# Half a unit of the next stage's projection ahead of the meeting at four seams of a two-layer encoder

## The chip, the cores and the metric

The kernel runs on one core of one Trainium2 chip. It is written by hand, one program for each engine, with semaphores between them. The metric is the device time of one launch in microseconds (us); the smaller, the better. Several runs are taken and their median counts.

## The reference

Two layers of an encoder over 1024 tokens of 1024 channels. Each layer projects the normalized input with one wide matrix `w_in` (1024 x 8464) and feeds three branches from it: windowed attention (a), differential attention over the full sequence (b), and a gated delta rule in both directions behind a short convolution (c). The three outputs are gated and merged.

```python
for l in range(DEPTH):                       # 2
    h = rmsnorm(x, norm_g[l])
    proj = einsum('bsd,de->bse', h, w_in[l])
    (a_q, a_k, a_v, a_z, b_q, b_k, b_v, b_z,
     c_qkv, c_z, c_b, c_a, gate_logits) = split(proj, offsets)
    o_a = windowed_gqa(a_q, a_k, a_v, a_sink[l], cos, sin)     # 8 heads, window 128
    y_a = (o_a * silu(a_z)) @ w_bo_a[l]
    o_b = diff_attention(b_q, b_k, b_v, lam, b_subln_g[l], lam_init, cos, sin)
    y_b = (o_b * silu(b_z)) @ w_bo_b[l]
    c_q, c_k, c_v = split(silu(centred_short_conv(c_qkv, c_conv_w[l])), 3)
    # beta and g from c_b, c_a; unit length for q and k
    o_c = rmsnorm(gated_delta_chunked(forward) + flip(gated_delta_chunked(backward)))
    y_c = (o_c * silu(c_z)) @ w_bo_c[l]
    gates = sigmoid(gate_logits)             # three of 1024 channels
    merged = gates[0] * y_a + gates[1] * y_b + gates[2] * y_c
    x = x + merged @ w_out[l]
return rmsnorm(x, final_g)
```

## The kernel before, in words

**Stages.** A layer is a chain of six blocks of code, one function each: `project(l)`, `attend_window(l)` (names with `win`), `attend_full(l)` (`diff`), `prepare(l)` (`prep`), `delta_rule(l)` (`delta`) and `merge_output(l)`. A small stage that loads x stands ahead of layer one, and one for the last norm behind layer two. Inside a block every engine has a program of its own (sync for DMA queues, gpsimd, tensor, scalar, vector). All engines meet at a block's end, and no engine starts on the next block before; in the profile TensorE's sequencer shows this at line 203. The four seams that the change touches are those from `project` to `attend_window`, from there to `attend_full`, on to `prepare`, and on to `delta_rule`.

**Units and halves.** Only the first columns of `proj` are made by `project`. The rest is cut in units of 128 columns (`U_BQ + k`, `diff_unit`, the gates' units), and TensorE makes them in the stages between, among each stage's own work ("side" work, class `Side`, lines 221 to 294). A unit for all 1024 tokens is two halves of 512 tokens. A half is 8 slices of the contraction, with three matmuls each, since float32 is computed as a sum of products of a high and a low part: 24 matmuls of 128x512 (`part`, line 266). The steps of a unit:
- `load`: SyncE loads the 1024 x 128 weights into `w_stage[k % 2]`.
- `split`: GpSimd makes `w_hi[k % 2]` (line 246) and `w_lo[k % 2]` (line 251), in four pieces each. In `prepare`, ScalarE makes the high part (`high`, line 1805) and GpSimd the low part (`low`, line 1691).
- `half`, or `part` slice by slice: TensorE accumulates a half in a bank of PSUM. It waits for `side_lo` (the unit is split) and for `side_out`: the half before it in the same bank has been read.
- `out`: ScalarE copies the bank into `ev[k % 2]` (line 281), and after a unit's second half issues its store to `proj` (line 285).

The last two units that a stage splits (`ahead=True`, or the numbers UNITS and above) belong to the next stage, which finds their semaphores set ahead by the numbers in `AHEAD`; with `SIDE_AHEAD_IN`, only one counts as split. `project` works on pairs of units of its own kind; its last loads and splits are those of the two units that `attend_window` begins with, and that stage's `split(1)` makes the second of them once more. The halves of `attend_window` and `attend_full` all go through bank 7 (`banks=(7, 7)`); in `prepare` and `delta_rule` the first half of a unit goes through bank 6 and the second through bank 7.

**TensorE's order in each stage.** The order is written out by hand; nothing is planned at run time.
- `attend_window`: halves 0 and 1, `turn_values` (transposes of the values, line 917), halves 2 and 3, then the steps: `scores(n)` (line 934), side parts, `turn`, `sum_values`, ... and `LAST` = 3 halves behind the last steps. GpSimd's order is split(1), three sines (`sine(r)`, line 883), split(2), and so on. `FIRST` = 4 counts the halves ahead of the steps.
- `attend_full`: `FIRST` = 3 halves, then steps of `scores(n)` (line 1317), side parts, `turn`, `sum_values` (line 1357); `LAST` = 5 halves at the end, between which `sum_squares` stands. The keys' parts that the scores read are made by ScalarE (`high`, line 1396) and VectorE (`low`, line 1505).
- `prepare`, for each of four heads: halves, `total` (sums of squares, line 1728), a half, `total`, halves, `products`, `turn` of k, a half, `turn` of v (line 1743), halves. ScalarE begins with high(1) and with a `tanh` (line 1774) among its evictions; GpSimd begins with low(1).
- `delta_rule`: `EARLY` = 10 halves, then four stages of `blocks` (line 2082) that solve the triangular systems from `delta_u` and its like, which are loaded back from memory (line 1962).

## Time and profile before

| | us |
|---|---|
| median of 3 runs | 2816.32 (2814.8 to 2816.42) |
| the profiled execution, its own time | 2818.19 |
| its span in the profile | 2816.4 |
| TensorE busy | 2684.4 (95%) |
| VectorE / GpSimd / ScalarE busy | 1473.7 / 1199.6 / 1153.8 |
| mean granted TensorE clock | 0.982 of full speed |

How to read it: times are microseconds from the span's start. PE is TensorE's matmuls, PEld its weight loads (which overlap them), PEq its sequencer; DVE is VectorE, ACT ScalarE, POOL GpSimd, and SPq or ACTq the DMA issues of SyncE or ScalarE. L266 is line 266 of the kernel. An operation is written out<-in, with the names of the program's buffers.

### The profile page before, as it was taken

How to read it: one execution, taken by the hardware profiler on the slowest of the kernel's cores; microseconds unless marked ns; L12 is line 12 of the kernel's file. 1: busy time of each engine (PE TensorE's matmuls, PEld its weight loads, DVE VectorE, ACT ScalarE, POOL GpSimd, SP SyncE). 2: the span in 40 equal slices, each digit the busy share in tenths (PEclk: the TensorE clock that was granted, in tenths of full speed). 3: DMA queues.
4: the chain of work that ended last, by engine and by line, in shares of the span. 5: the costliest groups of instructions: out<-in, count | busy, mean ns of one | idle time of the engine just before them, and what ended most of it. 6: DMA issues, size and time to landing. Idle time of an engine off the chain costs nothing. (4 is left out here: it accounts for less than half of the span.)

```text
span 2816.4 us, 39100 instructions
## 1 busy us (share of the span) xinstructions
PE 2684.4 (95%) x15158; PEld 2143.7 (76%) x15158; DVE 1473.7 (52%) x1835; ACT 1153.8 (41%) x1914; POOL 1199.6 (43%) x1108
## 2 busy tenths in 40 slices
PE   8989999999999999999999999899999999999998
PEld 4867767777778789878767777677777887897786
DVE  5136527777467343476240555277764764335752
ACT  3124424666365414342121344266663653244311
POOL 2464335443365450253434653444433654303633
PEclk9999999999999999999999999999999999999999
DMA  6253224231355555754243532433224564567532
GB/s 210 92 150 98 90 80 125 90 98 68 120 184 185 187 156 155 233 187 129 83 153 105 143 104 69 123 97 98 83 68 135 191 197 160 164 161 257 158 120 105
DMA packets 394072, 380.89 MB, mean 135 GB/s; under 512 B 90144, under 2 KB 332448, under 8 KB 393888
## 3 DMA queue, kind: packets, MB, share of 16 engines
q1 hardware_dynamic: 354912, 296.39, 34.8%
q10 hardware_dynamic: 38976, 82.00, 7.9%
q8 instruction: 121, 1.98, 0.3%
q14 instruction: 63, 0.52, 0.1%
HBM read 248.22 MB, written 130.09 MB: 134 GB/s over the span
## 5 line engine op out<-in xcount | busy, mean ns | idle before, releaser
L266 PE MATMUL pair<-h_hi,w_hi 128*128 128x512 f32 x1792 | 740.2, 413 | 75.0 <-PEq L203 39.9
L266 PE MATMUL pair<-h_lo,w_hi 128*128 128x512 f32 x1792 | 708.5, 395 | 0.0
L266 PE MATMUL pair<-h_hi,w_lo 128*128 128x512 f32 x1792 | 708.3, 395 | 0.0
L246 POOL TENSOR_TENSOR w_hi<-w_stage,masks 128x256 fp32r<-128x256 f32 x312 | 257.5, 855 | 642.7 <-PE pair L266 604.7
L266 PEld LDWEIGHTS pair<-h_hi,w_hi 128*128 128x128 f32 x1792 | 342.4, 191 | 197.0 <-issue 83.3
L266 PEld LDWEIGHTS pair<-h_hi,w_lo 128*128 128x128 f32 x1792 | 342.4, 191 | 75.6
L266 PEld LDWEIGHTS pair<-h_lo,w_hi 128*128 128x128 f32 x1792 | 343.3, 192 | 70.2 <-issue 5.3
L281 ACT ACTIVATE ev<-pair 128x512 f32<-128x512 f32 x224 | 132.8, 593 | 456.7 <-PE pair L266 455.7
L251 POOL TENSOR_TENSOR w_lo<-w_stage,w_hi 128x256 fp32r<-128x256 f32 x312 | 247.3, 823 | 6.1
L1691 POOL TENSOR_TENSOR w_lo<-w_stage,w_hi 128x256 fp32r<-128x256 f32 x128 | 149.5, 1197 | 170.5 <-ACT w_hi L1805 170.5
L1446 ACT ACTIVATE diff_p<-pair,diff_stat 128x1024 f32<-128x1024 f32 x128 | 142.9, 1117 | 126.4 <-DVE diff_stat L1549 122.4
L217 PE MATMUL pair<-h_hi,w_hi 128*128 128x512 f32 x512 | 158.5, 391 | 0.0
L217 PE MATMUL pair<-h_lo,w_hi 128*128 128x512 f32 x512 | 157.8, 389 | 0.0
L217 PE MATMUL pair<-h_hi,w_lo 128*128 128x512 f32 x512 | 157.6, 389 | 0.0
L1549 DVE TENSOR_REDUCE diff_stat<-pair 128x1 f32<-128x1024 f32 x128 | 150.1, 1214 | 1.3 <-PE pair L1317 1.0
L2401 POOL TENSOR_TENSOR w_lo<-w_stage,w_hi 128x512 fp32r<-128x512 f32 (+1 forms) x60 | 125.9, 2098 | 57.7 <-ACT w_hi L2458 54.2
L2399 POOL TENSOR_TENSOR w_hi<-w_stage,masks 128x512 fp32r<-128x512 f32 (+1 forms) x44 | 77.4, 1758 | 168.3 <-PE pair L217 147.7
L1032 ACT ACTIVATE win_s<-win_s,small 128x385 f32<-128x385 f32 (+1 forms) x128 | 74.7, 585 | 103.4 <-DVE small L1112 103.4
L1511 DVE TENSOR_TENSOR diff_a_lo<-pair,diff_a_hi 128x1024 fp32r<-128x1024 f32 x64 | 78.2, 1222 | 73.3 <-ACT diff_a_hi L1468 63.1
L535 POOL TENSOR_TENSOR w_hi<-w_stage,masks 128x1024 fp32r<-128x1024 f32 x20 | 47.6, 2381 | 157.0 <-PE pair L217 145.8
L1575 DVE SCALAR_TENSOR_TENSOR diff_p<-diff_p,diff_stat,diff_p 128x1024 f32<-128x1024 f32 x64 | 89.0, 1390 | 45.9 <-ACT diff_p L1455 45.7
L217 PEld LDWEIGHTS pair<-h_hi,w_hi 128*128 128x128 f32 x512 | 95.5, 188 | 21.3 <-issue 1.7
(288 smaller groups left out, 4894.7 us busy)
## 6 DMA issues: line engine op xcount, KB each, us to landing
w_stage<-in_w_in SPq DMA_DIRECT2D x132, 512.0 KB, 4.2
proj<-ev ACTq DMA_DIRECT2D x132, 512.0 KB, 2.7
gate<-proj SPq DMA_DIRECT2D x48, 512.0 KB, 3.7
prep_x<-proj SPq DMA_DIRECT2D x24, 512.0 KB, 4.1
resid<-xT SPq DMA_DIRECT2D x16, 512.0 KB, 6.2
diff_vx<-proj SPq DMA_DIRECT2D x16, 512.0 KB, 3.2
prep_g<-gc_rows SPq DMA_DIRECT2D x16, 512.0 KB, 5.0
qd_t<-prep_eg SPq DMA_DIRECT2D x16, 512.0 KB, 2.6
```

What stands on the lines that cost most here:

```text
L217: last = nc.tensor.matmul(pair[0:m, half, :], lhs[:, k, 0:m], rhs[:, k, half * HALF:(half + 1) * HALF], start=(k == 0 and n == 0), stop=(k ...
L246: last = nc.gpsimd.tensor_tensor(w_hi[s][:, part], w_stage[s][:, part], bcast(ones, PIECE), ALU.mult)
L251: last = nc.gpsimd.tensor_tensor(w_lo[s][:, part], w_stage[s][:, part], w_hi[s][:, part].bitcast(F32), ALU.subtract)
L266: last = nc.tensor.matmul(bank(self.banks[half]), a[s][:, c, :], b[:, c, w], start=(c == 0 and n == 0), stop=(c == KC - 1 and n == 2))
L281: nc.scalar.activation(ev[s][:, half * HALF:(half + 1) * HALF], bank(self.banks[half]), ACT.Tanh if gate else ACT.Copy, scale=0.5 if gate ...
L1446: nc.scalar.activation(p[c][:], flat(pairs[c]), ACT.Exp, bias=st[:, 0, c:c + 1], accum_out=st[:, 2, c:c + 1]).then_inc(q["exped"], 1)
L1511: nc.vector.tensor_tensor(a_lo[:, :, w], by_tile(pairs[2]), a_hi[:, :, w].bitcast(F32), ALU.subtract)\
L1549: nc.vector.tensor_reduce(st[:, 0, c:c + 1], flat(pairs[c]), AX_X, ALU.max, negate=True)\
L1575: nc.vector.scalar_tensor_tensor(out=p[0][:], in0=p[1][:], scalar=st[:, 4, 0:1], in1=p[0][:], op0=ALU.mult, op1=ALU.add).then_inc(q["mixed ...
L1691: last = nc.gpsimd.tensor_tensor(w_lo[s][:, part], w_stage[s][:, part], w_hi[s][:, part].bitcast(F32), ALU.subtract)
L2399: nc.gpsimd.tensor_tensor(hi, stage, bcast(ones, kc), ALU.mult).then_inc(q[f"w_hi{s}"], 1)
L2401: nc.gpsimd.tensor_tensor(lo, stage, hi.bitcast(F32), ALU.subtract).then_inc(q[f"w_lo{s}"], 1)
```

## The change

TensorE makes half 0 of the next stage's first unit at the end of the stage before, ahead of the meeting: a new function `lead`. The next stage's ScalarE evicts it first. The bank that holds it is given to `Side` as the first of `early`, and the first few halves of `attend_window` and `attend_full` go round three banks. `AHEAD` is changed so that each of the four stages finds both of its first two units split and one half summed. Where the stage before split one unit for the next (`attend_full`, `prepare`) it now splits two; the next stage's own split of unit 1 goes, and `FIRST` and `LAST` move by one.

```diff
+SIDE_AHEAD = {"side_in0": 16, "side_in1": 16, "side_hi": 2, "side_lo": 2, "side_sum": 1}
-AHEAD["win"] = SIDE_AHEAD_IN          (likewise "prep" and "delta"; "diff" had SIDE_AHEAD)
+AHEAD["win"] = dict(SIDE_AHEAD)
...
 class Side:
-    def __init__(self, l, q, per, banks=(7, 7)):
+    def __init__(self, l, q, per, banks=(7, 7), early=()):
+        self.bank_of = lambda n: early[n] if n < len(early) else banks[n % 2]
...
     part: (matmul and eviction use bank(self.bank_of(2 * k + half)))
+        n = 2 * k + half
+        late = 0 if self.bank_of(n) == self.bank_of(n - 1) else 1
+        pe.wait_ge(q["side_out"], START + turn * (2 * self.per) + max(n - late, 0))
...
+def lead(pe, into):
+    for c in range(KC):
+        for n, (a, b) in enumerate(((w_hi, h_hi), (w_hi, h_lo), (w_lo, h_hi))):
+            nc.tensor.matmul(bank(into), a[0][:, c, :], b[:, c, 0:HALF], start=(c == 0 and n == 0),
+                             stop=(c == KC - 1 and n == 2))
+LEAD_WINDOW, LEAD_FULL, LEAD_GATES = 6, 0, 6
 # project, TensorE, at the end
+    pe.wait_ge(q["w_lo0"], START + pairs_of_units + 1)
+    lead(pe, LEAD_WINDOW)
 # attend_window
-side = Side(l, q, UNITS)
+side = Side(l, q, UNITS, early=(LEAD_WINDOW, 7, 5, 7, 5))
-FIRST, LAST = 4, 3
+FIRST, LAST = 5, 2
-    split(1)                                   (GpSimd, ahead of the sines)
-    side_half(0)
     side_half(1); turn_values(); side_half(2); side_half(3)
+    side_half(4)
...
-    side_half(tail_half(2))
+    pe.wait_ge(q["side_lo"], START + UNITS + 1)
+    lead(pe, LEAD_FULL)
 # attend_full
+side = Side(l, q, UNITS, early=(LEAD_FULL, 7, 5, 7))
-FIRST, LAST = 3, 5
+FIRST, LAST = 4, 4
+    split(17)                                  (GpSimd, at the end)
-    for n in range(FIRST): side_half(n)
+    for n in range(1, FIRST): side_half(n)
...
-    side_half(tail_half(4))
+    pe.wait_ge(q["side_lo"], START + UNITS + 1)
+    lead(pe, LEAD_GATES)
     (ScalarE)
-    for n in range(2): side_out(n); high(0, n)
-    side_out(2)
+    side_out(0)
+    for n in range(2): side_out(n + 1); high(0, n)
+    side_out(3)
 # prepare: GpSimd low(1) and ScalarE high(1) go from the start, low(17) and high(17) stand at the end
-    half(0); half(1); h == 0: half(2), half(3)
+    h > 0: half(0), half(1); h == 0: halves 1 to 4
     total(h, 1)
-    half(2 if h else 4)
+    half(2 if h else 5)
     total(h, 0)
-    half(3 if h else 5); half(4 if h else 6)
+    half(3 if h else 6); h > 0: half(4)
     products(h); turn of k
-    h > 0: half(5)
+    half(5 if h else 7)
     turn of v
-    h > 0: half(6); half(7)
+    h > 0: half(6), half(7)
+pe.wait_ge(q["side_lo"], START + PREPARED + 1)
+pe.wait_ge(q["side_out"], START + 2 * PREPARED - 1)
+lead(pe, LEAD_GATES)
 # prepare, ScalarE, head 0: the halves' evictions follow the new order
-    out_half(0, 0); ...; tanh; ...; out_half(0, 3); ...; out_half(h, 4); out_half(h, 5)
+    out_half(0, 0); ...; tanh; ...; out_half(0, 3); ...; out_half(0, 4); ...; out_half(0, 5)
 # delta_rule
-    for k in range(1, N_GATE - PREPARED): split   (GpSimd)
+    for k in range(2, N_GATE - PREPARED): split
-    for n in range(EARLY): side_half(n)
+    for n in range(1, EARLY): side_half(n)
+    side_out(0)                                (ScalarE, first of all)
```

## Rows read from the trace of the kernel before

**Rows 1.** The page, part 1: busy time of each engine, share, instructions.

```profile
PE 2684.4 (95%) x15158; PEld 2143.7 (76%) x15158; DVE 1473.7 (52%) x1835; ACT 1153.8 (41%) x1914; POOL 1199.6 (43%) x1108
```

**Rows 2.** Waits of TensorE: waiting line <- releaser: total, times, longest.

```profile
PE pair L266 <- PEq L203: 39.9, 8, 6.2
PE pair L266 <- ACT ev L281: 29.2, 34, 3.9
...
PE pair L1743 <- ACT k_tok L1800: 2.4, 2, 1.2
```

**Rows 3.** Three windows: length, busy by engine, granted clock, DMA share, GB/s.

```profile
151.77:157.83 6.06, 6.06 (x14) 4.78 (x15) 0.00 (x0) 0.00 (x0) 2.07 (x3) 0.50 0.89 205
185.10:188.55 3.45, 3.45 (x8) 2.80 (x9) 0.83 (x2) 1.56 (x2) 3.37 (x5) 0.51 0.54 152
1540.07:1543.64 3.57, 3.57 (x9) 2.80 (x10) 0.00 (x0) 0.00 (x0) 0.00 (x0) 0.50 0.81 186
```

**Rows 4.** Time line of TensorE, seam one: start, duration, line, operation, [idle before].

```profile
151.77 0.77 PE L266 MATMUL pair<-h_hi,w_hi 128*128 128x512 f32 x1 [5.44 <-PEq L203]
...
166.62 1.03 PE L917 MATMUL pair<-masks,win_vx 128*128 128x128 f32 x8
...
180.84 0.38 PE L934 MATMUL pair<-win_hi,win_hi 64*128 64x256 f32 x2
...
185.10 0.80 PE L266 MATMUL pair<-h_hi,w_hi 128*128 128x512 f32 x1 [3.65 <-POOL w_lo L251]
```

**Rows 5.** Time line of GpSimd, seam one.

```profile
148.90 2.34 POOL L538 TENSOR_TENSOR w_lo<-w_stage,w_hi 128x1024 fp32r<-128x1024 f32 x1
...
161.53 3.87 POOL L883 TENSOR_TENSOR win_xr<-win_xr,sin 128x256 f32<-128x256 f32 x4
...
176.43 5.77 POOL L246 TENSOR_TENSOR w_hi<-w_stage,masks 128x256 fp32r<-128x256 f32 x4
```

**Rows 6.** The tile win_vx, its instructions and DMA to landing.

```profile
L1012 ACTq DMA_DIRECT2D win_vx<-proj x1: 445/445/445, 153.5 to 153.5; - x1
...
DMA to landing us min/median/max: 11.3/11.3/11.3
```

**Rows 7.** Time line of all engines, seam two.

```profile
412.94 2.76 POOL L246 TENSOR_TENSOR w_hi<-w_stage,masks 128x256 fp32r<-128x256 f32 x4 [7.47 <-PE pair L266]
...
419.04 0.76 PE L266 MATMUL pair<-h_hi,w_hi 128*128 128x512 f32 x1 [6.18 <-PEq L203]
...
437.12 1.25 DVE L1505 TENSOR_TENSOR diff_k_lo<-diff_xk,diff_k_hi 128x1024 fp32r<-128x1024 f32 x1 [1.13 <-ACT diff_k_hi L1396]
...
439.05 2.81 POOL L251 TENSOR_TENSOR w_lo<-w_stage,w_hi 128x256 fp32r<-128x256 f32 x4
...
440.02 0.73 PE L1317 MATMUL pair<-diff_k_hi,diff_q_hi 64*128 64x512 f32 x4
...
441.61 0.50 PE L266 MATMUL pair<-h_hi,w_hi 128*128 128x512 f32 x1
```

**Rows 8.** Time line of all engines, seam three.

```profile
755.55 0.60 ACT L281 ACTIVATE ev<-pair 128x512 f32<-128x512 f32 x1 [5.82 <-PE pair L266]
...
759.48 0.76 PE L266 MATMUL pair<-h_hi,w_hi 128*128 128x512 f32 x1 [3.97 <-PEq L203]
...
770.46 1.06 ACT L1774 ACTIVATE prep_t<-k_all 128x1024 f32<-128x1024 f32 x1 [0.54 <-DVE k_all L1888]
...
775.63 5.86 POOL L1691 TENSOR_TENSOR w_lo<-w_stage,w_hi 128x256 fp32r<-128x256 f32 x4 [12.35 <-ACT w_hi L1805]
...
784.11 1.88 PE L1728 MATMUL pair<-prep_t,masks 128*128 128x512 f32 x4
```

**Rows 9.** Time line of all engines, seam four.

```profile
977.92 0.77 PE L266 MATMUL pair<-h_hi,w_hi 128*128 128x512 f32 x1 [3.96 <-PEq L203]
...
1030.99 1.91 ACTq L1962 DMA_DIRECT2D delta_u<-solved  x4
...
1035.32 0.60 PE L2082 MATMUL pair<-delta_t,delta_qm 64*32 64x32 f32 x32
```

More of the change, by code:

```diff
@@ L152, in build_program @@
             "qd_put1"] + SIDE)
-        AHEAD["delta"] = SIDE_AHEAD_IN
+        AHEAD["delta"] = dict(SIDE_AHEAD)
         SIGNALS["delta"] = (["w_raw_in", "w_in", "zeroed", "w_set", "w_copied", "w_scaled", "w_solved", "kept",
@@ L222, in build_program @@
         class Side:
-            def __init__(self, l, q, per, banks=(7, 7)):
-                self.q, self.per, self.banks = q, per, banks
+            def __init__(self, l, q, per, banks=(7, 7), early=()):
+                self.q, self.per = q, per
+                self.bank_of = lambda n: early[n] if n < len(early) else banks[n % 2]
                 self.in_slot = [(per + 1 - s) // 2 for s in range(2)]
@@ L260, in part @@
                 if c == 0:
-                    late = 0 if self.banks[0] == self.banks[1] else 1
-                    pe.wait_ge(q["side_out"], START + turn * (2 * self.per) + max(2 * k + half - late, 0))
+                    n = 2 * k + half
+                    late = 0 if self.bank_of(n) == self.bank_of(n - 1) else 1
+                    pe.wait_ge(q["side_out"], START + turn * (2 * self.per) + max(n - late, 0))
                 w = slice(half * HALF, (half + 1) * HALF)
                 for n, (a, b) in enumerate(((w_hi, h_hi), (w_hi, h_lo), (w_lo, h_hi))):
-                    last = nc.tensor.matmul(bank(self.banks[half]), a[s][:, c, :], b[:, c, w], start=(c == 0 and n == 0),
+                    last = nc.tensor.matmul(bank(self.bank_of(2 * k + half)), a[s][:, c, :], b[:, c, w], start=(c == 0 and n == 0),
                                             stop=(c == KC - 1 and n == 2))
@@ L280, in out @@
                 act.wait_ge(q["side_sum"], START + turn * (2 * self.per) + (2 * k + half + 1))
-                nc.scalar.activation(ev[s][:, half * HALF:(half + 1) * HALF], bank(self.banks[half]), ACT.Tanh if gate else ACT.Copy,
+                nc.scalar.activation(ev[s][:, half * HALF:(half + 1) * HALF], bank(self.bank_of(2 * k + half)), ACT.Tanh if gate else ACT.Copy,
                                      scale=0.5 if gate else scale).then_inc(q["side_out"], 1)
@@ L890, in split @@
                             side.split(pool, 1, k - UNITS, ahead=True)
-                    split(1)
                     for r in range(3):
@@ L1154, in attend_full @@
                 UNITS = 4 * HEADS
-                side = Side(l, q, UNITS)
+                side = Side(l, q, UNITS, early=(LEAD_FULL, 7, 5, 7))
                 side_unit = lambda k: diff_unit(k // 4, k % 4)
@@ L1295, in _ @@
                     split(16)
+                    split(17)
                 @block.tensor
@@ L1359, in sum_squares @@
                         last.then_inc(q["total"], 1)
-                    for n in range(FIRST):
+                    for n in range(1, FIRST):
                         side_half(n)
@@ L1697, in mask @@
                         nc.gpsimd.tensor_tensor(G[d][:], G[d][:], bcast(beyond(d), NT), ALU.add).then_inc(q["masked"], 1)
-                    low(1)
                     for h in range(4):
@@ L1717, in _ @@
                         low(4 * h + 4)
+                    low(17)
                 @block.tensor
@@ L1747, in _ @@
                         half = lambda n: side.half(pe, 0, 4 * h + n // 2, n % 2)
-                        half(0)
-                        half(1)
-                        if h == 0:
-                            half(2)
-                            half(3)
+                        if h:
+                            half(0)
+                            half(1)
+                        else:
+                            for n in range(1, 5):
+                                half(n)
                         total(h, 1)
-                        half(2 if h else 4)
+                        half(2 if h else 5)
                         total(h, 0)
-                        half(3 if h else 5)
-                        half(4 if h else 6)
+                        half(3 if h else 6)
+                        if h:
+                            half(4)
                         products(h)
@@ L1809, in out_half @@
                         side_out(act, m)
-                        if m % 2 and (m + 3) // 2 <= PREPARED:
+                        if m % 2:
                             high((m + 3) // 2)
-                    high(1)
                     for h in range(4):
@@ L1831, in _ @@
                         to_exp(1, h)
-                        out_half(h, 2 if h else 4)
+                        if h:
+                            out_half(h, 2)
                         out_half(h, 3 if h else 5)
@@ L2050, in _ @@
                     last.then_inc(q["zeroed"], 1)
-                    for k in range(1, N_GATE - PREPARED):
+                    for k in range(2, N_GATE - PREPARED):
                         side.split(pool, 0, k)
@@ L2105, in blocks @@
                         last.then_inc(q["levels"], 1)
-                    for n in range(EARLY):
+                    for n in range(1, EARLY):
                         side_half(n)
@@ L2196, in _ @@
                     nc.scalar.activation(W[:, 1], RAW1, ACT.Copy).then_inc(q["w_copied"], 1)
-                    for n in range(EARLY):
+                    for n in range(1, EARLY):
                         if n == EARLY - 1:
```

24 lines of the change are left out of this document (9 added, 15 removed).

## The prediction

> **What bounds the kernel now.** I read the page first: TensorE is busy for 2684.4 of 2816.4 us, no other engine for more than 1474 [rows 1]. So TensorE's order of work is the path, and a change pays only by its pauses (132 us in all) or its clock. The view of waits then says where the pauses are [rows 2]: 39.9 us in 8 pauses behind the meetings of the engines (the sequencer's line 203), up to 6.2 each; 29.2 in 34 for a ScalarE eviction; and small ones, such as 2.4 for k_tok. Third, the windows behind those pauses: TensorE's granted clock is 0.50 of full speed, that is 1.2 instead of 2.4 GHz, for 6.06 us after the 5.44 us meeting pause, for 3.57 us after its twin in layer two, and for 3.45 us after a 3.65 us pause [rows 3]. Half of such a stretch is lost: 3.0, 1.8, 1.7 us. Last, the time lines of all engines around the four seams of layer one, to see which engine ended the stage and what TensorE waits for behind the meeting. The second layer repeats them.
>
> **What every seam gains and what it costs.** The change moves one half (24 matmuls) ahead of each of the four meetings of a layer. Such a half takes 5.45 us at full clock: ten of them between 977.92 and 1035.32 are 57.4 us, less 3.0 for the half clock, by ten [rows 9]. The number of matmuls in the program stays the same; what changes is pauses. Behind a meeting that TensorE ends itself, it should pause about 0.5 us: at the first seam GpSimd's split ended at 151.24 (148.90 + 2.34) and TensorE resumed at 151.77 [rows 4, 5]. But the half that is moved was also the filler under which the next stage's loads and splits ran. So each seam has to be followed until the next stage's own data stand in the way. I call the moment at which TensorE resumes r.
>
> **Seam one, projection to window attention.** Before, TensorE ends at 146.33 (151.77 - 5.44). The lead half runs until 151.8, next to the split which ends at 151.24, so r moves by +0.5 to 152.3. Behind r TensorE has halves 1, the turn of the values, 2, 3, 4 and then the scores. The values' load is issued at 153.5 and lands 11.3 us later, at 164.8 [rows 6], 165.3 after; TensorE is there at 157.8 and pauses 7.5 us, where before half 0 and half 1 covered it (turn at 166.62). It does the turn and two halves until about 180 and then wants unit 2, which GpSimd splits behind its three sines, from 176.43 on, and TensorE waited for it before too, until 185.10 [rows 4, 5]. Taking split(1) out of GpSimd's queue doesn't bring this forward. It ended just ahead of the first sine, at 161.53, whose input had landed just then (VectorE's cosine on the same input starts with it), and the later sines wait for their loads as well; I take 0, and the bound below is a split 5.7 us earlier (its cost), which no load supports. So half 4 starts at 185.6 against 185.1, and the scores of step 0 (0.6 us), done before in the cover of that pause, now stand behind it: 0.5 + 0.6 lost. The pause ahead of it grows from 3.65 to some 5.8 us; behind it I take 2.2 us lost to the half clock (between the rows' 1.8 and 3.0) against 1.7. Sum -1.6 us per layer, ends 0 and -3. The 5.44 us pause and its 3.0 us of half clock are gone, but come back as the pauses for values and unit 2.
>
> **Seam two, window to full attention.** Before: TensorE ends at 412.86 (419.04 - 6.18) and GpSimd's split of unit 17 only starts there (412.94), 5.6 us. After: that split starts at half 31's end and runs beside the values' sum (1.1 us) and the lead (5.45), 6.5 in all; the pause falls from 6.18 to 0.5, +5.7. Behind r before: three halves (one at half clock, two evictions waited for), scores at 440.02 = r + 21.0 [rows 7]. After: three halves on three banks take 16.4 us; but the low part of k comes from loads, sine, rotation and split: 437.12 + 1.25 = 438.4, r + 19.3. So a new pause of 2.9 us, then 1.6 us of scores (440.02 to 441.61), then half 4, whose unit GpSimd ends at 439.05 + 2.81 = 441.86 = r + 22.8 (it waited 0.4 for TensorE's half; 22.4 after). Before, half 3 started at 441.61 = r + 22.6. So +0.2 there, less 0.4 for what the clock may take: +5.5 per layer, ends +3.5 and +6.5.
>
> **Seam three, full attention to preparation.** Before, TensorE ends at 755.51 and ScalarE's eviction (755.55 + 0.60) and its store make the meeting wait: pause 3.97 [rows 8]. After, the store runs under the lead, and GpSimd's added split(17) starts with it: twice 2.8 us, the price of a split in rows 7, or 5.7 against 5.45; the pause is 0.8, +3.2. Halves 30 and 31 have the sum of squares between them, which hides an eviction wait of 0.75: it is among the 34 [rows 2]. Behind r before: four halves, total at 784.11 = r + 24.6. After: half 1 and 2 until r + 10.9; half 3 wants bank 7, which ScalarE empties only behind the tanh that starts at 770.46, r + 12.7: pause 1.8. Half 4 is of unit 2: its high part follows at r + 14.2, the low part takes GpSimd 5.86 beside VectorE's taps, r + 20.1: pause 2.0. Total at r + 25.5, 0.9 later. One half then stands between the turns of k and v, and the k_tok wait (2.4 in 2) goes: +1.2. Sum +4.2, ends +2 and +5.5.
>
> **Seam four, preparation to delta rule.** Pause 3.96 to 0.5: +3.4, and the 3.0 of half clock go. But this stage begins with halves 0 to 9 and then needs the solved blocks: VectorE's chain, a round trip through memory, and ScalarE's loads 1030.99 + 1.91 = 1032.90, landing some 1.5 us later, about r + 56.5 [rows 9]. TensorE came at r + 57.4, just behind. With nine halves it comes at r + 49.1. ScalarE, no longer held by half 8, can issue up to 1.6 us earlier: inputs at r + 55, pause 5.9 us, and 2.2 of half clock behind. Before: 3.96 + 3.0 = 7.0 of pause and clock; after: 0.5 + 5.9 + 2.2 = 8.6. So -1.7 per layer, ends 0 and -3.
>
> One rule bears on this. The rows show half clock behind the pauses of 3.65 and 5.44 us and full clock through the busy stretches [rows 3, 4]. The Trainium skill ("TensorE: Matmul & The Clock Gate", "HAM oscillation — how this bites in real kernels") has it that loads waited for between groups of matmuls make each group start slow, and its advice is to order the work so that the engine stays busy. By that the lead is right where it closes the pause and worth nothing where the pause only moves; the first of these, at every seam, is the first rival below.
>
> **Other edits at nothing.** Three early banks instead of one: the gain stands in seams two and three; the early evictions cost ScalarE the same 0.6 us each. Taking out high(1) and low(1) in the preparation and split(1) in the delta rule frees engines that nobody waits for there; what went in ahead of the meeting was counted at seam three, and at seam four high(17), low(17) is 0.6 + 0.5 + 1.06 + 2.8 = 5.0 us under a lead of 5.45 (if weights 17 came late it would cost their delay). The side work in the steps runs one half ahead and with the other parity; TensorE's waits there are evictions of 1.2 us and less, so I take 0, ends -2 and +2.
>
> **Sum.** Per layer -1.6 + 5.5 + 4.2 - 1.7 = 6.4; two layers 12.8, say 13. The profiled execution took 2818.19 us (span 2816.4 and 1.8 around it), so 2805.2; it stands 1.9 above the median of 2816.32, hence 2803.3 for the median.
>
> **Rivals.** (a) Full price: all eight pauses close to 0.5 (36 us), the half clock behind them is gone (about 2.7 each, 21), evictions too (5): 62 us, 2754. For it: rows 2. Against it: the loads and splits of seams one and four are just in time already. 4%. (b) Chain: slower. In window attention the first scores come 13 us later (194 against 181). If the chain scores, exp, turn, sum bounded this stage, its end would move by that, -26 in two layers, against the +16 that seams two to four bring: 2826. It decides from the point where that chain takes longer than a step of TensorE; against it, no wait for exp or turn stands among TensorE's large ones. 7%. (c) The new pauses of seams two and three each put TensorE at half clock (1.7 us, three times per layer) or the ends of seams one and four hold: gain about 3, 2813. 20%. (d) The pauses of seams one and four are milder, nothing lost there: gain 19, 2797. 15%. (e) The lead isn't done in the meeting's shadow, since something else holds TensorE (a split that its wait names comes late): the pause moves ahead of the lead, 0 to -5: 2818. 2%. My forecast, 2798 to 2809: 52%.
>
> Faster by over 0.2% (2810.7 and below; less than that can't be told from no change): 0.52 + 0.15 + 0.04 and a fifth of (c): 0.76. Same: the rest of (c) and half of (e), 0.16. Slower: 0.08. The range leaves out (a), (b) and the outer ends of (c) and (d): 2793 to 2815; the forecast's own is 2798 to 2809.
>
> **What would show it.** Line 266's waits for the meetings fall from 39.9 us to under 8. New in the waits: line 917 for the load of win_vx, 7 us in each layer; line 266 for w_lo by line 251, 6 us in each; line 2082 for the delta inputs, 5 to 6 in each; line 1317 for the low part of k, 3 in each; line 266 for w_lo by line 1691, 2 in each. Half clock behind the meetings is gone but stands behind the first three of these. The forecast is wrong if seam two's meeting doesn't come 5 us earlier, or if split(2) in window attention ends well ahead of TensorE.

## The result, and the profile after

The changed kernel takes 2832.33 us (median of 5 runs, 2828.0 to 2840.16) against 2816.32 (2814.8 to 2819.97, 5 runs): ratio 1.0061, 95% interval 1.0044 to 1.0078. It is slower by some 17 us where 13 us faster was forecast, and outside the range. Its profiled execution took 2837.72 us (span 2835.9), 5.4 above its median.

Line numbers below are mostly of the changed kernel: its lines 268, 252, 283, 1705, 1742 and 2098 are 266, 251, 281, 1691, 1728 and 2082 of the kernel before. First the page, part 1, of the changed kernel, for [rows 1]:

```profile
PE 2683.5 (95%) x15158; PEld 2143.0 (76%) x15158; DVE 1478.3 (52%) x1835; ACT 1153.4 (41%) x1914; POOL 1169.8 (41%) x1092
```

TensorE's busy time is the same (2684.4 before) with as many matmuls; the pauses are 152 us where they were 132. The waits of TensorE after, for [rows 2]:

```profile
PE pair L268 <- ACT ev L283: 24.1, 22, 1.7
PE pair L268 <- POOL w_lo L252: 22.1, 7, 6.2
PE pair L928 <- DMA win_vx<-proj: 13.8, 2, 6.9
PE pair L1742 <- ACT prep_t L1796: 9.8, 2, 4.9
PE pair L2098 <- DMA delta_u<-solved: 9.5, 2, 5.9
...
PE pair L1330 <- DVE diff_k_lo L1519: 6.2, 2, 3.1
PE pair L268 <- POOL w_lo L1705: 5.9, 4, 1.6
...
PE pair L268 <- PEq L203: 3.5, 8, 1.0
```

The meetings' 39.9 us are 3.5, as meant. In their place stand five waits that were forecast (win_vx, w_lo of unit 2, diff_k_lo, w_lo by line 1705, delta_u) and one that was not: 4.9 us in each layer for prep_t. Of the 22.1 us for w_lo by line 252, 4.7 (unit 7 of the window stage, in both layers) and 2.0 (a unit of the gates in layer two's delta rule) weren't forecast either, and of the 5.9 by line 1705, 1.36 in each layer (the second head's first half). Where they fall shows in the windows of the four stages, from one meeting to the next (columns as in [rows 3]); first the kernel before, then the changed one, layer one:

```profile
151.77:419.04 267.27, 253.30 (x1321) 191.25 (x1321) 129.01 (x198) 100.99 (x236) 127.35 (x160) 0.98 0.35 105
419.04:759.48 340.44, 323.37 (x1840) 258.66 (x1841) 224.50 (x273) 199.75 (x277) 145.93 (x155) 0.99 0.29 94
759.48:977.92 218.44, 213.26 (x992) 172.98 (x993) 133.44 (x101) 118.53 (x173) 114.12 (x80) 0.98 0.59 188
977.92:1174.00 196.08, 188.39 (x1873) 165.29 (x1873) 84.10 (x190) 68.17 (x166) 50.52 (x72) 0.98 0.57 165
```

```profile
153.03:424.25 271.22, 254.44 (x1321) 192.23 (x1321) 128.21 (x198) 100.76 (x236) 123.53 (x152) 0.97 0.34 103
424.25:763.14 338.89, 320.24 (x1840) 256.99 (x1841) 225.21 (x268) 199.84 (x276) 139.10 (x163) 1.00 0.30 94
763.14:985.73 222.59, 212.92 (x992) 171.40 (x993) 136.27 (x103) 118.33 (x173) 115.16 (x80) 0.99 0.58 185
985.73:1181.07 195.34, 181.51 (x1849) 159.04 (x1849) 83.39 (x190) 68.27 (x166) 44.74 (x64) 0.98 0.58 165
```

The first three stages do as many halves as before (each gives one away and takes one over) and end in a meeting that costs 3 to 6 us less, so each should be shorter. But window attention is 4.0 us longer and the preparation 4.2; only full attention is shorter, by 1.6. The delta rule, which does one half less (24 matmuls, 5.45 us), is 0.7 shorter. In layer two the four differences are +3.3, +0.2, +4.8 and +3.3. The last is not typical: of eight kernels below with the same delta rule seven took 192.7 to 195.1 us there, one 198.2, this one 199.1.

**Window attention, in the middle.** GpSimd and TensorE of the changed kernel, time line:

```profile
256.89 4.03 POOL L895 TENSOR_TENSOR win_xr<-win_xr,sin 128x256 f32<-128x256 f32 x4 [8.87 <-DMA win_xr<-proj]
260.88 2.83 POOL L247 TENSOR_TENSOR w_hi<-w_stage,masks 128x256 fp32r<-128x256 f32 x4
263.79 3.88 POOL L252 TENSOR_TENSOR w_lo<-w_stage,w_hi 128x256 fp32r<-128x256 f32 x4
...
267.72 0.50 PE L268 MATMUL pair<-h_hi,w_hi 128*128 128x512 f32 x1 [2.26 <-POOL w_lo L252]
```

And GpSimd at the same place before:

```profile
250.32 3.90 POOL L883 TENSOR_TENSOR win_xr<-win_xr,sin 128x256 f32<-128x256 f32 x4 [9.25 <-DMA win_xr<-proj]
...
258.07 2.94 POOL L251 TENSOR_TENSOR w_lo<-w_stage,w_hi 128x256 fp32r<-128x256 f32 x4
```

GpSimd's last sine waits for a load in both kernels, and the split of unit 7 is queued behind it. Before, that split ended 6 us ahead of its use (261.01 and 266.99). The sine's load goes with the stage's steps, and with 5 halves instead of 4 ahead of the steps they begin a half later: the sine starts 6.6 us later and the split ends 6.7 us later (267.67), while TensorE wants the unit 1.5 us sooner (265.46).

**Full attention, in the steps.** The other parity moves GpSimd's gating (line 1280) from behind a split (572.37 in the trace before, behind the split that starts at 564.81) to beside VectorE's mixing (line 1589):

```profile
564.99 2.40 POOL L1280 TENSOR_TENSOR diff_o<-diff_o,diff_zt 128x1024 f32<-128x1024 f32 x1 [2.42 <-DVE diff_o L1536]
565.27 3.20 DVE L1589 SCALAR_TENSOR_TENSOR diff_p<-diff_p,diff_stat,diff_p 128x1024 f32<-128x1024 f32 x1
...
572.52 0.50 PE L268 MATMUL pair<-h_hi,w_hi 128*128 128x512 f32 x1 [1.02 <-ACT ev L283]
```

VectorE's operation has a median of 1.28 us over its 64 places and takes 3.20 here: it ends 1.08 us behind GpSimd's (568.47 and 567.39), as if it had hardly begun before. The maximum, the exp and the eviction behind it are late, and TensorE pauses 1.02 us where it paused 0.16. This happens twice per layer.

**Preparation, second head.** ScalarE, SyncE and TensorE of the changed kernel, three stretches of the time line (the first row of the first and of the last is of the first head):

```profile
782.52 1.06 ACT L1796 ACTIVATE prep_t<-k_all 128x1024 f32<-128x1024 f32 x1
...
827.61 1.06 ACT L1823 ACTIVATE w_hi<-w_stage 128x1024 fp32r<-128x1024 f32 x1 [9.59 <-DMA w_stage<-in_w_in]
829.47 1.05 ACT L1792 ACTIVATE prep_t<-prep_yq 128x1024 f32<-128x1024 f32 x1
830.42 1.05 ACT L1796 ACTIVATE prep_t<-k_all 128x1024 f32<-128x1024 f32 x1
```

```profile
822.77 0.43 SPq L237 DMA_DIRECT2D w_stage<-in_w_in  x1
```

```profile
788.70 1.88 PE L1742 MATMUL pair<-prep_t,masks 128*128 128x512 f32 x4
...
831.52 1.14 PE L1742 MATMUL pair<-prep_t,masks 128*128 128x512 f32 x1 [4.93 <-ACT prep_t L1796]
```

And ScalarE and TensorE in the kernel before, at the same place:

```profile
825.41 1.05 ACT L1778 ACTIVATE prep_t<-k_all 128x1024 f32<-128x1024 f32 x1
...
827.05 1.45 PE L1728 MATMUL pair<-prep_t,masks 128*128 128x512 f32 x3
```

Before, the square was ready at 826.46 and TensorE came at 827.05: no pause, but a margin of 0.6 us, and no view of waits shows a margin. From the meeting on, TensorE did ten halves ahead of this total. Now one of them is done ahead of the meeting and nine are left, while the square comes at r + 68.3 instead of r + 67.0 (r is TensorE's start in the stage, 763.14 and 759.48). TensorE itself is there at 826.59, r + 63.4 instead of r + 67.6. So of the pause 4.1 us are the missing half and 1.3 the later square, less the margin of 0.6.

**The clock.** Five windows right behind pauses of the changed kernel (values, unit 2, unit 7, prep_t, delta_u):

```profile
165.59:167.60 2.01, 2.01 (x9) 2.01 (x10) 1.23 (x1) 0.39 (x1) 1.60 (x2) 0.50 1.08 277
185.17:190.10 4.93, 4.93 (x12) 3.91 (x13) 0.00 (x0) 0.00 (x0) 4.85 (x8) 0.52 0.38 106
267.72:271.50 3.78, 3.78 (x10) 2.99 (x11) 3.12 (x5) 2.46 (x6) 3.78 (x4) 0.59 0.68 171
831.52:835.20 3.68, 3.68 (x5) 1.60 (x6) 3.61 (x4) 2.98 (x4) 1.67 (x2) 0.54 1.14 350
1041.13:1046.00 4.87, 4.87 (x42) 3.94 (x43) 0.00 (x0) 1.07 (x4) 0.00 (x0) 0.50 0.79 205
```

The first stretch goes on at 0.50 to 169.48, 3.89 us in all. So each of these pauses brings its own stretch at or near 1.2 GHz: 1.5 to 2.4 us lost (the length times one less the granted clock). The one of only 2.26 us, ahead of unit 7, costs 1.5 of that. The Trainium skill ("TensorE: Matmul & The Clock Gate", "HAM oscillation — how this bites in real kernels") has waits for loads between groups of matmuls make the next group start at the low clock, and the trace agrees.

### The profile page after: what moved, and what is told of

Same layout as the page of the kernel before. It is cut to its first block and busy times, and to the rows that moved or that the text cites. A ratio compares the mean times of both kernels' runs of the same rounds, so it can differ in the third digit from the quotient of the medians.

```text
span 2835.9 us, 39076 instructions
## 1 busy us (share of the span) xinstructions
PE 2683.5 (95%) x15158; PEld 2143.0 (76%) x15158; DVE 1478.3 (52%) x1835; ACT 1153.4 (41%) x1914; POOL 1169.8 (41%) x1092
## 5 line engine op out<-in xcount | busy, mean ns | idle before, releaser
L268 PE MATMUL pair<-h_hi,w_hi 128*128 128x512 f32 x1728 | 712.9, 413 | 56.7 <-ACT ev L283 24.1
L268 PE MATMUL pair<-h_lo,w_hi 128*128 128x512 f32 x1728 | 680.5, 394 | 0.0
L268 PE MATMUL pair<-h_hi,w_lo 128*128 128x512 f32 x1728 | 680.4, 394 | 0.0
L247 POOL TENSOR_TENSOR w_hi<-w_stage,masks 128x256 fp32r<-128x256 f32 x304 | 245.3, 837 | 586.5 <-PE pair L268 536.5
L268 PEld LDWEIGHTS pair<-h_hi,w_hi 128*128 128x128 f32 x1728 | 328.5, 190 | 173.5 <-issue 63.4
L268 PEld LDWEIGHTS pair<-h_hi,w_lo 128*128 128x128 f32 x1728 | 328.6, 190 | 72.7
L268 PEld LDWEIGHTS pair<-h_lo,w_hi 128*128 128x128 f32 x1728 | 329.2, 191 | 68.4 <-issue 6.3
L252 POOL TENSOR_TENSOR w_lo<-w_stage,w_hi 128x256 fp32r<-128x256 f32 x304 | 222.1, 762 | 6.0
L1705 POOL TENSOR_TENSOR w_lo<-w_stage,w_hi 128x256 fp32r<-128x256 f32 x128 | 150.1, 1202 | 165.0 <-ACT w_hi L1823 165.0
L217 PE MATMUL pair<-h_hi,w_hi 128*128 128x512 f32 x512 | 158.4, 391 | 0.0
L217 PE MATMUL pair<-h_lo,w_hi 128*128 128x512 f32 x512 | 157.7, 389 | 0.0
L217 PE MATMUL pair<-h_hi,w_lo 128*128 128x512 f32 x512 | 157.7, 389 | 0.0
L1589 DVE SCALAR_TENSOR_TENSOR diff_p<-diff_p,diff_stat,diff_p 128x1024 f32<-128x1024 f32 x64 | 97.1, 1517 | 46.1 <-ACT diff_p L1470 46.0
L1119 DVE SCALAR_TENSOR_TENSOR win_s<-pair,band 128x768 f32<-128x768 f32 (+1 forms) x64 | 56.9, 890 | 109.3 <-PE pair L945 109.2
```

The lines of the kernel that those rows point to most:

```text
L217: last = nc.tensor.matmul(pair[0:m, half, :], lhs[:, k, 0:m], rhs[:, k, half * HALF:(half + 1) * HALF], start=(k == 0 and n == 0), stop=(k ...
L247: last = nc.gpsimd.tensor_tensor(w_hi[s][:, part], w_stage[s][:, part], bcast(ones, PIECE), ALU.mult)
L252: last = nc.gpsimd.tensor_tensor(w_lo[s][:, part], w_stage[s][:, part], w_hi[s][:, part].bitcast(F32), ALU.subtract)
L268: last = nc.tensor.matmul(bank(self.bank_of(2 * k + half)), a[s][:, c, :], b[:, c, w], start=(c == 0 and n == 0), stop=(c == KC - 1 and n ...
L1589: nc.vector.scalar_tensor_tensor(out=p[0][:], in0=p[1][:], scalar=st[:, 4, 0:1], in1=p[0][:], op0=ALU.mult, op1=ALU.add).then_inc(q["mixed ...
L1705: last = nc.gpsimd.tensor_tensor(w_lo[s][:, part], w_stage[s][:, part], w_hi[s][:, part].bitcast(F32), ALU.subtract)
```

## The experiments

All ratios are to the kernel before, run beside each kernel on the same chip; its medians there were 2813.6 to 2816.6 us. Every kernel does the whole computation.

**One seam at a time.** Each has the lead at one seam, with what the change did in the stages on its two sides; the rest is as before.

> The lead half at seam one alone (projection to window attention), with the window stage's own order of halves as before (4 halves ahead of the steps, 3 behind). Theory A (what seam one gives is what the forecast said, and the loss in the middle of the window stage comes from the half that the steps run ahead, which this kernel does not do): the pauses for the values (7 us) and for unit 2 (about 6 us) stand in place of 5.44 us, 0.75 and 3.65, nothing waits in the middle: +0 to +3 us for both layers, 2816 to 2819. Theory B (the new pauses cost what they cost in the changed kernel, w_lo pause near 268 us included): +6 to +9, 2822 to 2825.

> The lead half at seam two alone (window to full attention), with the full attention stage as in the changed kernel. Theory A: the meeting's pause falls from 6.2 to 0.3 us, 0.6 us is lost ahead of the first scores, and about 2.2 us in each layer to evictions in the steps that come late in the new parity: about 3.7 us gained per layer, 2809. The forecast's own size for this seam: 5.5 per layer, 2805. Theory B (the gain shows nowhere, since a later chain takes it back): 2816.

> The lead half at seam three alone (full attention to preparation). Theory A (the preparation is bound at the second head's total by the chain of VectorE and ScalarE, which starts at the meeting: TensorE had just enough halves to cover it, and the half done ahead is one less): the pause of 4 us goes at the meeting but 4.9 us come back at the second head's total with half clock behind it, and the meeting itself is 5.45 - 3.3 later: 3 to 5 us lost per layer, 2822 to 2826. The forecast's size (+4.2 gained per layer): 2808.

> The lead half at seam four alone (preparation to delta rule). The forecast's size: 1.7 us lost per layer, 2820, with a pause of some 6 us for delta_u in each layer. Theory A: the same for the pause, and in one layer or the other 1 to 3 us more behind it (a late split of the gate units, or late step values): 2819 to 2825. Rival: nothing lost at all, since the pause replaces the meeting's one for one: 2816.

| lead at | ratio | 95% interval | us, both layers | forecast |
|---|---|---|---|---|
| seam one | 1.0003 | 0.9994 to 1.0013 | +1 | +3 |
| seam two | 0.9982 | 0.9971 to 0.9993 | -5 | -11 |
| seam three | 1.0039 | 1.0024 to 1.0055 | +11 | -8 |
| seam four | 1.0014 | 1.0005 to 1.0024 | +4 | +3 |

The us are (ratio - 1) x 2815. The sum is +11. The forecast has seams one and four right; seam two gives half of it; seam three has the wrong sign. Theory A is nearest at all four; seam two gives a little less than it says and seam three costs a little more. In the kernel with seam three alone the windows of the two stages (full attention, preparation) read

```profile
420.35:763.80 343.45, 329.53 (x1864) 263.49 (x1864) 225.02 (x268) 199.71 (x276) 151.56 (x163) 0.99 0.29 93
763.80:984.57 220.77, 207.52 (x968) 167.02 (x969) 136.13 (x103) 117.23 (x172) 112.28 (x76) 0.99 0.58 186
```

Full attention is 3.0 us longer, with a half more (5.45) and the cheaper meeting. The preparation does a half less and is still 2.3 us longer than before.

**The window stage's order.**

```diff
 # split7_first, GpSimd           # window_4_3
 split(6)                         -FIRST, LAST = 5, 2
+split(7)                         +FIRST, LAST = 4, 3
 sine(5)                          (half 4 in the steps, one more half at the end)
-split(7)
```

> The changed kernel, but GpSimd splits unit 7 of the window stage ahead of its last sine (it stood behind it). Theory A (the 2.3 us pause of TensorE in the middle of the window stage, at 267.7 and 1660.9 in the trace of the changed kernel, is this split, late behind the sine since the steps run one half ahead; half clock of 1.7 us follows): both pauses go, 8 us less than the changed kernel, ratio to the kernel before about 1.003 (the changed one had 1.0061). Rival (the unit's weights or the buffer come late, not the order): the pause stays, 1.006.

> The changed kernel, but with 4 halves ahead of the window stage's steps and 3 behind, as before, so that the steps do not run one half ahead. Theory A: the same pauses in the middle go by the other way, and the first scores fall back into the cover of the pause for unit 2 (0.6 us more): 8 to 9 us less than the changed kernel, ratio 1.003. Rival (the loss in the middle comes from the gain at the seam itself): 1.006.

Measured: 1.0040 (1.0027 to 1.0053) and 1.0035 (1.0022 to 1.0048) against the changed kernel's 1.0061. The pauses at 267.7 and 1660.9 are gone in both profiles. The intervals overlap a little with the changed kernel's (1.0044 to 1.0078), but two different edits that remove the same two pauses agree: the order in the steps cost 6 to 7 us in all. With the four seams' 11 that is the 17 us measured.

**The preparation: three trials that missed, one that hit in part.**

```diff
 # prep_shifted: every half from head 0's end on one place earlier (TensorE, ScalarE)
 # weights5_first, SyncE, head h > 0
+weights(4 * h + 1)
 put_queries(h - 1); load(h + 1, 1); put_products(h - 1, 0)
-weights(4 * h + 1)
 # squares_first, ScalarE
 square(1, 1)
+high(5)                           (stood behind half 7's eviction)
```

> The changed kernel, but in the preparation TensorE does every half from head 0's end on one place earlier (half 8 behind head 0's turns, halves 9 and 10 ahead of the second head's first total, and so on), so that as many halves lie ahead of that total as before the change. Theory A (the chain of ScalarE and VectorE sets that total, and a half fewer lay ahead of it): the pauses of 4.9 us and the half clock behind them (1.5 us) go, 13 us less than the changed kernel, ratio 1.0015. Rival (the halves, one place earlier, wait for their own splits, high parts behind ScalarE's tanh and low parts behind GpSimd's masks): the pause is split over several, 1.004 to 1.006.

> The changed kernel, but in the preparation SyncE issues the load of unit 4h+1's weights ahead of its other issues for head h (it stood behind the stores of the products of the head before). Theory C (the pause of 4.9 us at the second head's total is this load: it is issued at 822.8 behind seven stores that wait for VectorE's product, lands at 827.5, ScalarE's high part of unit 5 waits for it, and the tanh and the square that TensorE's total needs stand behind it on ScalarE): the load goes out at about 815.5, lands by 821, the square is done when VectorE's convolution and silu are (about 826.9), TensorE pauses under 0.6 us there; 12 us less than the changed kernel, ratio to the kernel before 1.002 (the changed one 1.0061). Theory A as first put (VectorE's and ScalarE's own work is the chain): the pause stays, 1.006.

> The changed kernel, but ScalarE makes the high part of unit 5 in the preparation behind the square of the second head's k instead of ahead of it; the load stays where it was. Theory C: the total's input is ready at about 827 as well, so the pause of 4.9 us goes, but unit 5 is now split later: its half (the third of the second head) may wait 1 us; 10 to 12 us less than the changed kernel, ratio 1.002 to 1.0025. Theory A: no change, 1.006.

Measured: 1.0099 (1.0084 to 1.0114), 1.0047 (1.0033 to 1.0060), 1.0073 (1.0059 to 1.0086). With one more half ahead of the total, that half waits 5.9 us for unit 5's low part and two more waits of 1.3 appear. With the square first, the pause goes to the same half:

```profile
PE pair L268 <- POOL w_lo L1705: 16.7, 6, 5.4
...
PE pair L1742 <- ACT prep_t L1796: 0.6, 2, 0.3
```

With the load first the wait for prep_t falls from 9.8 to 3.9 us, yet the kernel gains some 4 us where 12 were expected, and the intervals overlap. So the load was one link and not the whole cause: behind it ScalarE waits for VectorE's convolution.

> seams_1_2_3, but in the preparation's first head both totals stand one half earlier (behind halves 3 and 4, as many halves into the stage's own order as before the change), and ScalarE takes the first root ahead of half 4's eviction. Theory E (the square is ready at 20.4 us into the stage, the total waits until 25.5 behind half 4, which waits for its split; from there the chain of roots, decays and products is late until the second head): the chain moves forward by up to 5 us, the pauses at the second head's total (2.0 and 1.6 us and their half clock, about 5 us per layer) shrink: ratio 0.992 to 0.9935. Rival (VectorE is busy without a break from the first head's silu to the second head's, so its own work sets the second head's total): 0.995 as seams_1_2_3.

> The changed kernel with one edit: the preparation's first head does both totals one half earlier (and ScalarE its first root ahead of half 4's eviction). Theory E: the 4.9 us pause at the second head's total shrinks to under 1 us in both layers, with the half clock behind it; the gain that this edit brought in the combination was 0.0056, so 1.0061 falls to 1.000 to 1.001. Rival (it needs the earlier load of unit 5's weights too, since ScalarE's high part of that unit waits for it ahead of the square): the pause stays at 3 us or more, 1.003 to 1.005.

```diff
 # head 0, TensorE (the changed kernel: halves 1 to 4, total, 5, total, 6)
-for n in range(1, 5): half(n)
+for n in range(1, 4): half(n)
 total(0, 1)
+half(4)
 total(0, 0)
+half(5); half(6)
 # ScalarE: to_root(1, 0) ahead of out_half(0, 4)
```

Measured: in the combination 0.9951 became 0.9895 (0.9877 to 0.9912); in the changed kernel, with this edit alone, 1.0061 became 1.0035 (1.0023 to 1.0047). The preparation there, window of layer one:

```profile
766.07:984.14 218.07, 212.83 (x992) 171.57 (x993) 133.59 (x103) 118.67 (x173) 115.57 (x80) 0.99 0.59 188
```

It is 218.1 us instead of 222.6 (218.4 instead of 223.0 in layer two), and the 4.93 us pause is 1.35, with the load of unit 5 left where it was. But a new one stands in the first head: TensorE now comes to the first total before its square is ready and waits 2.1 us in each layer. The waits for prep_t together:

```profile
PE pair L1742 <- ACT prep_t L1795: 7.2, 4, 2.1
```

The gain in the time was expected at 15 us and is some 7, in the band of the rival, though its pause of 3 us isn't there: the place was right, the size was not. In the combination the two ratios say 16 us, but they come from different chips; by the profiles the stage is 4.5 and 4.0 us shorter there too (218.45 to 213.97, 218.24 to 214.24), 8.5 to 9 us in all in both cases. That lies inside what the first pair of ratios allows and at the edge of the second, so it is the better figure. The first total stood behind half 4, and half 4 waited for the split of unit 2; the square it needs was ready 5.1 us sooner (782.52 + 1.06, total at 788.70). Behind that total stand the root, the decays, the products, their stores and the load of unit 5: this chain ends in the second head's square, and it begins a half earlier now.

**The delta rule.** `EARLY, LATE = 11, (1, 4)` instead of `10, (1, 3, 5)`.

> The changed kernel, but in the delta rule 10 halves (11 with the one done ahead) instead of 9 stand ahead of the first blocks, and one less in the chunks' steps (behind chunks 1 and 4 instead of 1, 3 and 5). Theory A (at seam four the half done ahead is the one that covered the round trip of the solved blocks through memory): the pause for delta_u (5.9 and 3.6 us) and its half clock go, 10 us less, unless the steps now lack a half: then TensorE waits in the steps for about half of that. Ratio 1.0025 to 1.0045. Rival (the pause's place does not matter, all fillers are needed where they stand): 1.006.

Measured 1.0063 (1.0050 to 1.0076), no gain. The waits for delta_u fell from 9.5 to 4.5 us, but TensorE waits for splits (line 252) nine times instead of seven, 23.5 us instead of 22.1, and the rest of the difference is not found; the profiled executions differ by more than that.

**Seam one's far side: the order of the loads.**

```diff
 # SyncE
+weights(2)
 load_plain(sp, 0); load_rotated(sp, 1); ...; load_z
-weights(2)
 # GpSimd
+split(2)
 sine(0..2)
-split(2)
 # TensorE, FIRST, LAST = 6, 1
-half 1, turn_values, halves 2, 3, 4
+halves 1, 2, 3, turn_values, halves 4, 5
```

> Leads at seams two and three only, window stage, start of it and delta rule as before the change, and the load of unit 5's weights first in the preparation. If the ledger holds: seam two alone measured 0.9982; seam three alone 1.0039 with both of the preparation's long pauses (4.9 us and 1.5 of half clock in each layer, 0.0045), so without them 0.9994; together 0.9976, some 7 us faster than before: 2807 where before stands at 2813.7. Rival (the preparation's pause comes back at the next head, seam three stays a loss): 0.9995 to 1.001.

> As seams_2_3, with the lead at seam one as well and the window stage's start arranged for it: SyncE loads unit 2's weights first, GpSimd splits it ahead of the sines, TensorE does halves 1, 2, 3, the turn of the values, 4 and 5 ahead of the steps (6 with the one done ahead), and unit 7 is split ahead of the last sine. Theory D (the pauses of 6.9 and 5.8 us at seam one come from the order of the loads, unit 2's weights landing 23 us into the stage): both go, some 2 us of waiting for the first scores remain; 5.4 + 3.65 + 3 us of half clock are gained against before, 10 us per layer less 2: ratio 0.992. Rival (the sines, 2.5 to 5 us later, set the first scores, and the steps, two halves ahead, wait for their splits elsewhere): 0.996 to 1.000.

> seams_1_2_3 without the lead at seam three and with the preparation as before the change. If seam three costs alone what it costs in the combination (1.0006 against 0.9982 for seam two alone, 0.0024): ratio 0.9951 - 0.0024 = 0.9927, some 2796 where before stands at 2816.5. Rival (the seams are not additive, and seam three is neutral once the rest is in place): 0.995.

> The lead at seam one alone, with the window stage's start as in seams_1_2_3 (unit 2's weights loaded first and split ahead of the sines, 6 halves ahead of the steps). In seams_1_2_3 the window stage took 258.9 us where it took 267.3 before; of the 8.4 us the meeting at its end (seam two's lead) gives 0.4. So 8 us per layer: ratio 0.9943. Rival (part of that gain needs the other leads): 0.996 to 0.998.

> No lead at all: the kernel before, but with unit 2's weights loaded first in the window stage, split ahead of the sines, no repeated split of unit 1, halves 0 to 3, the turn of the values and half 4 ahead of the steps, and unit 7 split ahead of the last sine. Theory D (the order of the loads is the gain at seam one's far side; the lead only gives the meeting's pause): TensorE's waits of 1.9 and 3.7 us and the half clock behind them go, the meeting's pause of 5.4 us stays: 5 to 7 us per layer less 0.6 for the first scores: ratio 0.996 to 0.998. Rival (order and lead each give nothing without the other): 1.000.

> prep_total_earlier with the lead at seam four as well, that is all four leads of the change with the window stage's start, the load of unit 5's weights and the first head's totals put right. If seam four costs what it did alone (0.0014): ratio 0.991. Rival (the preparation ends with room, and the earlier end gives the delta rule's round trip more cover): 0.988 to 0.989.

| kernel | leads | loads first | load 5 first | total earlier | ratio | 95% interval |
|---|---|---|---|---|---|---|
| seams_2_3 | 2, 3 | | yes | | 1.0006 | 0.9997 to 1.0015 |
| loads_first_no_lead | none | yes (5, 2) | | | 0.9974 | 0.9965 to 0.9983 |
| seam1_loads_first | 1 | yes | | | 0.9922 | 0.9907 to 0.9937 |
| seams_1_2 | 1, 2 | yes | | | 0.9920 | 0.9902 to 0.9937 |
| seams_1_2_3 | 1, 2, 3 | yes | yes | | 0.9951 | 0.9937 to 0.9964 |
| prep_total_earlier | 1, 2, 3 | yes | yes | yes | 0.9895 | 0.9877 to 0.9912 |
| all_four | 1 to 4 | yes | yes | yes | 0.9922 | 0.9908 to 0.9935 |

The tile of the staged weights says why, first in the changed kernel, then in seam1_loads_first:

```profile
L237 SPq DMA_DIRECT2D w_stage<-in_w_in x1: 432/432/432, 158.1 to 158.1; - x1
...
DMA to landing us min/median/max: 17.7/17.7/17.7
```

```profile
L237 SPq DMA_DIRECT2D w_stage<-in_w_in x1: 367/367/367, 153.7 to 153.7; - x1
...
DMA to landing us min/median/max: 4.9/4.9/4.9
```

Issued behind the twenty other loads with which SyncE and ScalarE begin the stage, unit 2's weights landed at 175.8 (175.5 before the change); issued ahead of SyncE's others, at 158.6. The window stage of loads_first_no_lead is 264.2 us (267.3 before), that of seam1_loads_first 256.9 with a half (5.45 us) less in it. So the order of loads, with the splits and halves arranged for it, is worth 7 us in all without a lead, as expected; and the lead that gave nothing alone (1.0003) brings 15 more on top of it, with one half more ahead of the steps (16 for the whole against before were expected, 22 measured). The waits say where they come from:

```profile
PE pair L268 <- PEq L203: 37.2, 8, 5.4
PE pair L268 <- ACT ev L283: 30.6, 30, 4.5
```

```profile
PE pair L268 <- PEq L203: 24.3, 8, 4.1
PE pair L268 <- ACT ev L283: 22.6, 30, 1.7
PE pair L268 <- POOL w_lo L252: 12.0, 3, 6.2
```

The first two lines are of loads_first_no_lead, the other three of seam1_loads_first. The meeting's pause goes (5.4 to 0.3 in each layer, 1.3 more at the stage's end), with its half clock, and the pause for the values doesn't come back in its place, since three halves stand ahead of the turn. But the pause for a split isn't gone, as theory D of seams_1_2_3 had it: it has moved from unit 2 to unit 3 (4.96 us at 188.44, 6.21 at 1565.73) where the kernel without a lead waits 4.5 for an eviction. What would remove it wasn't tried. The seam two lead adds next to nothing there (0.9922 and 0.9920): with one half left behind the window stage's steps, the meeting was 3.9 us in seam1_loads_first rather than 6.2. The other expectations: seams_2_3 came out at its rival, so the earlier load of unit 5 doesn't save seam three; seams_1_2_3 lies between its two; seams_1_2, on another chip, agrees that seam three still costs there (0.9920 to 0.9951). The rival for prep_total_earlier (VectorE's own work sets the second total) fell: in its profile TensorE no longer waits for prep_t at that total. With the totals moved, the lead at seam three is worth some 7 us (0.9920 to 0.9895, though the intervals overlap). The lead at seam four costs in the combination too (0.9895 to 0.9922, expected 0.0014). The best kernel is prep_total_earlier: 2787.33 us (2782.64 to 2793.27) where before has 2816.52, against both kernels of the case.

## Why the prediction was wrong

- **The meetings** were right: in layer one 5.4, 6.2, 4.0 and 4.0 us of pause became 0.3, 0.3, 0.7 and 0.3. Both signs that the prediction named for being wrong (seam two's meeting, split(2) in window attention) looked at places that went as forecast; neither would have shown the error.
- **Seam one** was right in its working: pauses of 6.86 and 5.75 us (7.5 and 5.8 forecast), half clock behind both, net about nothing (1.6 us per layer lost forecast, 0.4 measured with the steps' order as before). The remark that taking split(1) out brings unit 2 no earlier held too, though not by the sines alone: the unit's load lands at 175.5, within 1 us of their end.
- **Seam two**, "+5.5 per layer": pauses of 3.09 and 1.79 us behind it where the working has 2.9 and 1.5. Alone it gave 2.5 per layer; the late evictions in the steps (next point but one) are 2 of the 3 us that lack, the rest I can't place.
- **Seam three**, "Sum +4.2": the step "One half then stands between the turns of k and v, and the k_tok wait goes: +1.2" ended the working there, in the first head. The pauses ahead of the first total, 1.48 and 1.59 us, were near the 1.8 and 2.0 of the forecast, and so was the total's delay of 0.9 us; but I followed TensorE only that far. At the second head's total the margin was 0.6 us, TensorE came there a half poorer, and lost 4.93 us and the slow stretch (1.7). It could have been read: square ready 826.46, total at 827.05. The k_tok wait did go. total_earlier_only shows that the chain which this pause waits for begins at the first total, put behind the half that waits: with the total a half earlier the pause is 1.35.
- **"The side work in the steps runs one half ahead and with the other parity ... so I take 0, ends -2 and +2"** failed twice. In window attention a split queued behind a load-bound sine lost its 6 us margin: 3 to 4 us per layer, shown by split7_first and window_4_3. In full attention two evictions per layer come 0.85 us later, with 0.4 in small pieces 2.1 us in all; that the shift of GpSimd's gating causes this is read from the trace and wasn't tried by itself. I looked at what TensorE waited for, not at what it nearly waited for. The reason given was also misread: two evictions in the steps of full attention were waited for longer than 1.2 us before the change (1.70 at 459.96, 1.44 at 697.89).
- **Seam four** was right: 1.7 us per layer lost forecast, 2.0 measured, pause 5.88 us for delta_u in layer one (5.9 forecast) and 3.61 in layer two, where a late split had held TensorE for 1.96 before.
- **Rival (b)**, the one that was slower, was priced at 2826 by the chain of scores. That chain never showed; the slower result came from margins used up at three places.

In us for both layers: forecast -13; measured +17. Of the 30 between, seam three is 19, the order in the window's steps 7, seam two 6; seam one gives 2 back, and singles and sum agree within their intervals. The chances ahead of the sum are off by 0.01 (those for faster add to 0.75, those for the same to 0.17).

## What to carry to other kernels

A filler that is done ahead of a meeting is missing behind it: before moving it, list for each later instruction of the bound engine when its inputs were ready, not only where it waited, and follow this until the first place with room. Then move what feeds those places first (a weight load ahead of the stage's other loads, a total ahead of the half that waits for a split); the same lead that gave nothing brought 15 us after that. A half that waits for its split must not stand ahead of an instruction that starts a chain.

## What the hardware showed that was not expected

- A weight load of 0.5 MB lands 17.7 us after its issue behind the twenty loads with which the stage begins, and 4.9 us after it when it is issued ahead of them.
- VectorE's 128x1024 operation on two inputs in SBUF takes 3.20 us instead of 1.28 when a GpSimd operation of 2.40 us started 0.28 us ahead of it, and ends 1.08 us behind it. The row shows this as a longer operation, not as a wait. The Trainium skill ("SBUF — State Buffer", "SBUF: two separate sides") has the two engines share one pair of ports, held by the one that starts first for its whole instruction; the row agrees.
- A pause of only 2.26 us (267.72) is followed by 3.8 us at a mean granted clock of 0.59, and costs 1.5 us more.
